# The odd in-projection of a two-layer trunk, reordered and unrolled, with the indexer beside it

## The reference, cut to what matters

```
def odd_mixer(h, rel_bias, w_in, w_out, qk_g):
    proj = h @ w_in                       # [256, 4688]
    q, k, v, iq, ik, iw = split(proj, (2048, 512, 512, 1024, 64, 16))
    q = rms_norm(q.reshape(B, S, 16, 128), qk_g[0])
    k = rms_norm(k.reshape(B, S, 4, 128), qk_g[1])
    iq, ik = rope on the first 32 of 64 dimensions of each index head, and of the index key
    iw = iw * 16 ** -0.5
    # dsa_attention, per query t:
    rel = relu(einsum('bqhd,bkd->bqhk', iq, ik))
    score = einsum('bqhk,bqh->bqk', rel, iw), NEG above the diagonal
    idx = top_k(score, 64)
    attention of 16 heads in 4 key groups over the 64 chosen keys, with a relative bias
    return o @ w_out
```

## Time and profile before

| | us |
|---|---|
| median of 3 runs | 2156.24 |
| lowest, highest | 2148.58, 2157.21 |
| profiled execution | 2157.78 |
| its span, first to last instruction | 2156.1 |

### The profile page before, as it was taken

One profiled execution on the slowest core, in us unless ns is written; L12 is line 12 of the kernel. 1 busy time (PEld: TensorE's weight loads), 2 busy tenths in 40 slices (PEclk: granted clock), 3 DMA queues, 4 the chain that ended last, 5 costly groups with the idle time before them and its releaser, 6 DMA issues.

```text
span 2156.1 us, 35615 instructions
## 1 busy us (share of the span) xinstructions
PE 1966.7 (91%) x11596; PEld 1689.7 (78%) x11596; DVE 1558.4 (72%) x2425; ACT 1057.9 (49%) x2310; POOL 202.9 (9%) x317
## 2 busy tenths in 40 slices
PE   3189979888999999999999999779999999999998
PEld 2067765566789999997777777648789999998787
DVE  4987752655868888888786787587876777778554
ACT  1155524543555554556445555326555555556543
POOL 2210000333100000000010000014100000000000
PEclk9599979788999999999999999769999999999999
DMA  8979975445668888886885899546857777776565
GB/s 330 412 269 325 311 243 173 141 152 176 225 236 277 267 280 273 273 275 191 300 320 167 315 324 322 164 159 212 278 186 240 221 242 222 222 221 177 178 190 179
DMA packets 210820, 521.19 MB, mean 242 GB/s; under 512 B 24945, under 2 KB 38770, under 8 KB 185874
## 3 DMA queue, kind: packets, MB, share of 16 engines
q1 hardware_dynamic: 180578, 316.17, 45.9%
q0 software_dynamic: 28032, 201.44, 25.5%
q10 hardware_dynamic: 2096, 2.12, 0.3%
HBM read 517.52 MB, written 2.12 MB: 241 GB/s over the span
## 4 chain that ended last, share of the span: by engine, by line
PE 79%; DVE 11%; DMA 5%; ACT 3%; issue 1%; SPq 0%; DVEq 0%; ACTq 0%; POOLq 0%
PE ps L1001 11%; PE ps L997 11%; PE ps L998 11%; PE ps L885 10%; PE ps L881 10%; PE ps L882 10%; DVE acc L1546 5%; PE ps L722 2%; PE ps L1057 2%; DVE ring_lo L1621 1%; PE ps L1049 1%; PE ps L931 1%; DMA ring<-in_od_w_in 1%; PE ps L932 1%; PE ps L935 1%
## 5 line engine op out<-in xcount | busy, mean ns | idle before, releaser
L1621 DVE TENSOR_TENSOR ring_lo<-ring,ring_hi 128x512 fp32r<-128x512 f32 (+1 forms) x1152 | 743.0, 682 | 322.8 <-ACT ring_hi L1150 320.6
L1150 ACT ACTIVATE ring_hi<-ring 128x512 fp32r<-128x512 f32 (+1 forms) x1152 | 687.2, 621 | 568.1 <-DMA ring<-in_ffn_w_up 228.0
L997 PE MATMUL ps<-hT_hi,ring_hi 128*128 128x256 f32 x2048 | 513.2, 283 | 1.6 <-PE ps L1001 0.8
L998 PE MATMUL ps<-hT_lo,ring_hi 128*128 128x256 f32 x2048 | 508.2, 280 | 0.0
L998 PEld LDWEIGHTS ps<-hT_lo,ring_hi 128*128 128x128 f32 x2048 | 388.1, 189 | 0.0
L997 PEld LDWEIGHTS ps<-hT_hi,ring_hi 128*128 128x128 f32 x2048 | 385.6, 188 | 2.4 <-issue 1.8
L1001 PE MATMUL ps<-hT_hi,ring_lo 128*128 128x256 f32 x2048 | 329.6, 282 | 2.4 <-DVE ring_lo L1621 2.4
L1001 PEld LDWEIGHTS ps<-hT_hi,ring_lo 128*128 128x128 f32 x2048 | 279.6, 188 | 2.6 <-DVE ring_lo L1621 2.6
L1546 DVE SCALAR_TENSOR_TENSOR acc<-aring,cs_now,acc 128x2048 f32<-128x2048 f32 x106 | 249.3, 2352 | 5.8 <-DMA aring<-in_ada_w 0.2
L882 PE MATMUL ps<-ring_hi,hT_lo 128*128 128x512 f32 (+2 forms) x640 | 249.0, 390 | 0.0
L622 POOL DMA_DIRECT2D aring<-in_ada_w x176 | 94.1, 535 | 1383.2 <-DVE acc L1546 1360.4
(11 more groups left out here) (230 smaller groups left out, 2111.0 us busy)
## 6 DMA issues: line engine op xcount, KB each, us to landing
aring<-in_ada_w POOLq DMA_DIRECT2D x176, 1024.0 KB, 6.6
ring<-in_ffn_w_up SPq DMA_DIRECT2D x512, 256.0 KB, 3.0
ring<-in_ffn_w_down SPq DMA_DIRECT2D x256, 256.0 KB, 3.2
ring<-in_od_w_in SPq DMA_DIRECT2D x128, 256.0 KB, 4.8
ring<-in_ev_w_in SPq DMA_DIRECT2D x96, 256.0 KB, 5.4
first_ring<-in_ada_w POOLq DMA_DIRECT2D x16, 1024.0 KB, 6.8
ring<-in_ev_w_out SPq DMA_DIRECT2D x64, 256.0 KB, 3.3
ring<-in_od_w_out SPq DMA_DIRECT2D x64, 256.0 KB, 3.3
```

What stands on the lines that cost most here:

```text
L997: nc.tensor.matmul(o[q], hi, hT_hi[:, kt, :], start=start, stop=False, skip_group_check=True)
L998: nc.tensor.matmul(o[q], hi, hT_lo[:, kt, :], start=False, stop=False, skip_group_check=True)
L1150: ins = nc.scalar.activation(out_, in_, f, **kw)
L1621: put(v.tensor_tensor(ring_lo[:, g, part], ring[:, g, part], ring_hi[:, g, part].bitcast(F32), ALU.subtract), lo_ok)
```

## The change

The odd in-projection is written out without a hardware loop, in the order of `OD_BLOCKS`: 512 index-query columns, the other 592 index columns as two blocks of 296, the keys, four blocks of queries, the values. Each of the nine blocks has 16 units. Squares are taken only of keys and queries. The indexer's steps are placed at unit numbers i = 0 to 143 of the three engines' streams. PE's `beside(i)` has the index key's transpose at 59, a pair of index heads at 62, 65, ... 83, and the key transposes at 112. ACT has the pair copies and relus at 65 to 89. DVE has the rotations at 23, 27, 54, 56 and 58, the head sums from 69 to 91, the mask at 92, the rounds of top-k at 93, 95, ... 107, `selm` at 109, and the scaling of the blocks at 80, 96, 112, 128 and behind the last unit. The warming products are gone.

The keys' transposes are stored in `od` itself (`dsa_kT`). The order of the adaLN blocks is new. For n = 2 all 48 are in the list, the gate's first. Eight gate blocks of n = 2 come in the down-projection of n = 1 (`EARLY_GATE`), for which that sublayer's gate moves from `acc` to `hT` (`gate_cols`). Its own last 16 blocks and these 8 are spread from about its unit 18 to unit 123. The in-projection takes 20 (`OD_ADA`), attention 17 (three of four steps), the output projection 3.

```diff
+OD_BLOCKS = ((O_IQ, NB), (O_IQ + NB, 296), (O_IQ + NB + 296, 296), (O_K, NB), (0, NB), (NB, NB), (2 * NB, NB), (3 * NB, NB), (O_V, NB))
+OD_NORMED = (3, 4, 5, 6, 7)
+EARLY_GATE = 8
+OD_ADA = (6, 9, 12, 15, 18, 21, 30, 33, 36, 39, 42, 45, 48, 62, 110, 114, 118, 124, 130, 134)
...
-        MOD_PASSES = (3, 4, 4, 4)
+        MOD_PASSES = (3, 4, 0, 4)
...
+        def unit_in_step(n_sub, m):
+            return m % 2 == 1 if n_sub == 0 else m % 4 != 3
...
-            with sp.Fori(0, 4) as i:
-                for b in range(2):
-                    matrix(PLAN["od_in"] + KT * b, od_w_in[0], KT, i * (2 * NB) + b * NB, NB, i * (2 * KT))
-            matrix(PLAN["od_in"] + 8 * KT, od_w_in[0], KT, 8 * NB, O_COLS - 8 * NB)
+            for j, (c0, n) in enumerate(OD_BLOCKS):
+                matrix(PLAN["od_in"] + KT * j, od_w_in[0], KT, c0, n)
...
+                if n == 1:
+                    for args in rest:
+                        load(*args)
+                    pool.wait_ge(gate_red.handle, GATE_SUMS[1] + 1)
+                    clear(2, (2,))
+                    rest = [(first_mod(2) + j, 2, t, k) for j, (t, k) in enumerate(MOD_REST[2][:EARLY_GATE])]
...
+                def index_logits(hh):
+                    if hh >= 2:
+                        pe.wait_ge(irel.handle, hh - 1)
...
+                def beside(i):
+                    if i == 59:
+                        pe.wait_ge(irope.handle, 3)
...
+                    p, at = divmod(i - 62, 3)
+                    if at == 0 and 0 <= p < IDX_H // 2:
+                        if p + 1 < IDX_H // 2:
+                            pair_T(p + 1)
+                        pe.wait_ge(ik_ok.handle, 1)
+                        pe.wait_ge(iq_ok.handle, p + 1)
+                        index_logits(2 * p)
+                        index_logits(2 * p + 1)
...
+                for j, (c0, n) in enumerate(OD_BLOCKS):
...
+                    for u in range(KT):
+                        beside(KT * j + u)
+                        rows_block("od_in", KT * j, KT, n, 2 * (j % 2), h_parts, part=(u, u + 1))
...
-                warm(16, 0)
-                pe.wait_ge(irel.handle, IDX_H)
...
+                for i in range(AHEAD, len(OD_BLOCKS) * KT):
+                    low("od_in", i, w=UK * OD_BLOCKS[i // KT][1])
...
+                    p, at = divmod(i - 69, 3)
+                    if at < 2 and 0 <= p < IDX_H // 2:
+                        head_sum(2 * p + at)
+                    if i == 92:
+                        mask_sums()
+                    r, at = divmod(i - 93, 2)
+                    if at == 0 and 0 <= r < TOPK // 8:
+                        top_round(r)
...
+                    if i in OD_ADA:
+                        rest_unit(2)
+                scale_block(OD_NORMED[-1])
```

More of the change, by code:

```diff
@@ L649, in _ @@
                     for m in range(len(att.units)):
-                        if m % 2 == 1 and rest:
+                        if unit_in_step(n, m) and rest:
                             load(*rest.pop(0))
@@ L1463, in odd_mixer @@
                         act.wait_ge(idx_mm.handle, 2 * p - 2)
-                    run(iq_ok, iqT[:, p % 2, :], ps[:, p % 2, 0:S], ACT.Copy)
-                    for e in range(2):
-                        hh = 2 * p + e
-                        act.wait_ge(idx_mm.handle, hh + 1)
-                        if hh >= 2:
-                            act.wait_ge(isum.handle, hh - 1)
-                        run(irel, rel[:, hh % 2, :], ps[:, 2 + hh % 4, 0:3 * P], ACT.Relu)
-                attention(ODA, "od_out")
+                    run(iq_ok, iqT[:, p % 2, :], ps[:, 4 + p % 2, 0:S], ACT.Copy)
@@ L1473, in up_tile @@
+                run(None, root[:, :], ones[:, 0:1], ACT.Exp)
+                blk(len(OD_BLOCKS) - 1)
             def up_tile(f, before, r, s, extra=0):
@@ L1720, in more @@
                         low(name, u)
-                        if due(u - units, 2 * units, late):
-                            rest_unit(n)
+                        if u < 4 * units - 4 and due(u - units, 3 * units - 4, late):
+                            rest_unit(n if rest_at[n] < len(MOD_REST[n]) else n + 1)
                 more(units, units + AHEAD + 4)
@@ L1938, in odd_mixer, with key_and_weights, head_sum @@
+                def key_and_weights():
+                    lane.after()
+                    put(v.tensor_scalar(od[:, :, O_IW:O_COLS], od[:, :, O_IW:O_COLS], IDX_H ** -0.5 * IDX_D ** -0.5, None, ALU.mult), irope)
+                    for e in range(2):
+                        put(v.tensor_copy(ikd[:, :, e * IDX_D:(e + 1) * IDX_D], od[:, :, O_IK:O_IW]), irope)
+                def head_sum(hh):
                     dve.wait_ge(irel.handle, hh + 1)
@@ new lines, in scale_block @@
+                def scale_block(j):
+                    jj, c0 = OD_NORMED.index(j), OD_BLOCKS[j][0]
+                    dve.wait_ge(od_sq.handle, 9 * jj + 9)
+                    put(v.reciprocal(st[:, 8 * jj:8 * jj + 8], st[:, 8 * jj:8 * jj + 8]))
+                    lane.after()
+                    for t in range(ST):
+                        scale_heads(od[:, t, c0:c0 + NB].rearrange("p (h d) -> p h d", h=4),
+                                    st[:, 8 * jj + 4 * t:8 * jj + 4 * t + 4], 4, od_nrm)
@@ new lines, in odd_in @@
+                sums_cleared(2)
+                for i in range(AHEAD, len(OD_BLOCKS) * KT):
+                    low("od_in", i, w=UK * OD_BLOCKS[i // KT][1])
+                    if i in (23, 27):
+                        dve.wait_ge(proj_out.handle, 7 + 1)
+                        rope_heads((i - 23) // 4, 0)
+                    if i in (54, 56):
+                        dve.wait_ge(proj_out.handle, 7 + 3)
+                        rope_heads((i - 54) // 2, 8)
+                    if i == 58:
+                        for t in range(ST):
+                            rope_key(t)
+                        key_and_weights()
+                    p, at = divmod(i - 69, 3)
[6 more added lines that the diff above has]
+                        top_round(r)
+                    if i == 109:
+                        lane.after()
+                        put(v.tensor_scalar(selm[:, :], iwk, TAKEN / 2, NEG, ALU.is_gt, ALU.mult), sel_ok)
+                    if i >= 74 and (i - 74) % KT == 0:
+                        mean_squares(OD_NORMED[(i - 74) // KT])
+                    if i >= 80 and (i - 80) % KT == 0:
+                        scale_block(OD_NORMED[(i - 80) // KT])
+                    if i in OD_ADA:
+                        rest_unit(2)
```

243 lines of the change are left out of this document (142 added, 101 removed).

## The result

The changed kernel takes 2126.07 us, the median of 4 runs (2118.95 to 2133.6), beside 2156.72 us for the kernel before in the same session. The ratio is 0.9866, with a 95% interval of 0.9818 to 0.9913: about 30 us faster. The forecast was 2103 us, 53 us faster, and its range ended at 2125. So the direction was right, and the gain came out little more than half as large.

A forecast was written before the change was run, and what follows sets the result against it. The prediction took the 59.3 us serial stretch to be bound by DVE. Removing it, with +2.7 in-projection, +3.5 attention and 0 down-projection, gave -53 us: 2103 us as a median, range 2088 to 2125.

The forecast's parts named there:

- The serial stretch: Between the odd in-projection's last product and the first attention transpose: 59.3 us without weight products, forecast to leave PE's path.
- The down-projection before it: Down-projection ahead of the odd stage: 24 accumulations in 106 units instead of 16 in 64, priced 0 (-3 to +6).
- Attention: With the output projection: +1 steady part, +1 start, +2 last steps, -0.5 output projection; sum +3.5 us (0 to +14).
- own sign of being wrong: Wrong if index-stretch PE waits exceed 10 us, clock leaves 1.00 after unit 16, or down-projection lengthens over 6 us.
- unrolled code change no instruction's size: 0: Gate columns in hT, keys written back and unrolled code: 0, hidden under PE; without that cover each below 1.5 us.
- The narrow stretch: Odd in-projection's 32 units of 296 columns with 8 accumulations: 38 us, 12 us lost; bounds 26 and 45 us.
- the 37 us scaled from the even stage: Narrow units: the even in-projection's 1.21 us a unit, scaled by bytes to 1.15 us, times 32.
- the stall before 1193: Odd in-projection's start: first accumulation no longer waits until 1190.18 for a late-requested block, -2.4 us.
- Index work: PE beside the in-projection's products: 26 transposes about 3 us, 16 heads' logits 6.4 us; 9.5 us in all (9 to 16).
- The upper bound, 0.83: PE's index logits: an attention unit with the same products and two more took 0.83 us, the bound per head.
- Handovers: Index steps passing between PE, ACT and DVE in the in-projection: 5 us allowed, bounds 0 and 16 us.
- the one of 2121: Rival: narrow stretch 45 us and handovers 16 us, both at upper bounds: +18, 2121 us; chance 0.20.

## Why the forecast was right in kind and too large

**Right.** The serial stretch went off PE's path whole, as forecast, top-k included. The down-projection before it lost 1.2 us, against 0. In the wide units from 1260 us to attention the clock stayed at 1.00. Attention kept its step and, with the output projection, lost 2.5 us, against 3.5, but that is luck in part: +1 was meant for the steady steps and +2 for the last, and both took exactly what they took before. The whole loss lies in the first steps, 2.9 us where +1 was meant, and the clock, which the forecast took to no longer begin at the half, fell there to 0.51 for 10 us behind PE's waits. By the forecast's own sign of being wrong, a clock that leaves 1.00 after unit 16, this part of it was wrong. The landing time of the 1 MB blocks in narrow units held too, 7.2 us in the even stage and 7.3 in the new stretch.

**The step that failed is one of the edits costed at nothing: "unrolled code change no instruction's size: 0".** It named as its cover that the work is hidden under PE, and bounded it by 1.5 us. No instruction grew, but unrolling moved all of TensorE's code behind it. The loop of the second up-projection came to lie over eight blocks of 256 instructions instead of seven, and the second and third pass load it again: 12.0 us, in a stage that the prediction didn't look at. Putting the loop at slot 0 gives the 12 us back, slots 176 and 208 show the boundary, and slot 224 gives the stalls to the kernel before. The trace of before did show code being fetched (64 packets), but none of its rows could say at which slot the loop would land; the honest price would have been 0 or some 10 us (the size is known only from these runs), with a chance for each.

**The narrow stretch: right mechanism, size off.** It was priced 38 us and took 45.3, the upper bound that I had written for it, and 42 to 46 in the other executions with these places. Two numbers beneath it were off. It moved 14.0 MB (45.3 us x 310 GB/s) and not 13.2: nine blocks are asked for in it, and wide weight blocks for the units behind it. And the 37 us scaled from the even stage took all of that stage's bytes as moved within it: 428 KB in 1.21 us would be 362 GB/s, where its own row says 300, so a part must have landed before. At 300 GB/s 13.2 MB take 44 us; I had then taken 38, below even the 41 us that 13.2 MB at 325 give. What the price by bytes doesn't show is why PE feels it: accumulations stand in order on DVE, each late block delays three lows, and PE waits (12.4 us). From unit 30 on the blocks are one per three units, denser than in the even stage, where they are one per four. With four blocks in the stretch it takes 31 us.

**The start: 3.4 us.** I took the stall before 1193 for one of waiting for a block and let it vanish. The trace of before shows no such wait: DVE comes from other work and begins the accumulation at once, at 1190.18. It is the accumulation itself, 2.35 us ahead of a low, that holds PE, and it still does (PE waits 1.3 us before 1193.59 instead of 2.4). About 1.4 us of the 3.4 are a mistake in the sum: it took 2.4 us for the stall off units priced at 1.38 us each, which held no stall. From unit 6 at 1189.64 before, ten units without a stall reach 1203.4, not the 1202.0 of the forecast; it was 1205.45.

**Index work: 2 us more than forecast**, 11.5 against 9.5, within its bounds. The reading of 0.40 us a head, halved from a stretch at the half clock (0.50 from 1395 to 1400 us), was close to the 0.43 of a pair issued together. The upper bound, 0.83, is what a head costs alone. **Handovers:** about 6 us of the 150 are neither products nor index work, against 5; PE waits for DVE in 3.2 of them, and the clock is 0.83 from 1250 to 1260.

Of the rivals, the one of 2121 (narrow stretch and handovers both at their upper bounds) is nearest to the time, but its second half did not happen; the 12 us of code took its place. The range held no case for code at all, and ended 1 us short.

## What to carry to other kernels

When a change adds or removes unrolled code, price where the loops behind it come to lie: count the body of each long loop, compare the packets of the instruction queue before and after (64 and 85 here), and fix the loop's place if a pass is loaded more than once. Spread large side transfers over the stretches whose products are long, not over those that already move the most bytes per product (the narrow stretch took 45.3 us with nine blocks asked for in it, 31.3 with four), and look at what stands in order behind the instruction that waits for them. Do not load the first steps of a pipeline whose steady steps have room: here attention lost 2.9 us with 6.0 us of PE's waits and a clock of 0.51 over 10 us; with accumulations in half of the steps the waits were 3.5 us and the clock 0.83. A loss in a stage that the change doesn't touch is not noise by that alone: here it was 12.0 to 12.8 us in three executions of the changed kernel.

## What the runs showed of the hardware

- TensorE's loop of 1604 instructions is fetched once while its body spans seven blocks of 256 (slots 0 and 176: 375.7 us, 67 and 68 packets) and, without a hint for its branch, again in each pass over eight (slots 208 and 224: 383.9 and 383.8 us, 86 and 83 packets). A turn of the loop then costs 4 to 6 us (8.2 to 12.8 us over its two turns). With the hint, at what its packets say is the changed kernel's own place, it was 375.4 us and 67 packets.
- The granted clock fell beside some of these stalls and not beside others: the changed kernel showed 0.90 and 0.80 in two windows of 17 us and lost 12.0 us; the kernel before, with stalls of the same kind, stayed at 1.00 and lost 8.5, and the changed kernel with slot 208 showed 0.90 and 0.90 and lost 8.2.
- In attention's first steps it was 0.51 over 10 us with 6.0 us of PE's waits for DVE, and 0.83 with 3.5 us. In the narrow stretch one execution had 0.89 and another 1.00 with about the same waits (12.4 and 12.7 us), so waits alone do not tell when it falls.
- Logits over 64 rows: two heads in different halves of the rows took 0.86 us together and 1.63 us when issued apart. That the halves run side by side is read from the timeline; no kernel here tested it by itself.
